# The first projection stage takes its column pairs in another order: q and k first instead of v first

## What is computed

```python
def rope(x, pos):
    ...
    x1, x2 = xf[..., :half], xf[..., half:]
    return jnp.concatenate([x1 * cos - x2 * sin, x1 * sin + x2 * cos], axis=-1).astype(x.dtype)

def retention_layer(h, s0, pos, w_in, head_norm, w_out):
    proj = h @ w_in
    qk = RET_HEADS * RET_DK
    q = proj[..., :qk].reshape(b, L, RET_HEADS, RET_DK)
    k = proj[..., qk:2 * qk].reshape(b, L, RET_HEADS, RET_DK)
    v = proj[..., 2 * qk:2 * qk + RET_VW].reshape(b, L, RET_HEADS, RET_DV)
    gate = proj[..., 2 * qk + RET_VW:]
    q = rope(q, pos)
    k = rope(k, pos) * (RET_DK ** -0.5)
    o, s_new = chunked_linear_recurrence(q, k, v, log_a, s0)
    ...
    return (o * jax.nn.silu(gate)) @ w_out, s_new
```

## Time and profile before

| | |
|---|---|
| median of 3 runs | 2247.02 us (2246.4 to 2247.16) |
| profiled execution | 2246.4 us, its span 2244.6 us |
| PE busy | 2090.1 us, 93% of the span |
| DVE busy | 1264.9 us, 56% |
| ACT busy | 857.7 us, 38% |
| POOL busy | 386.6 us, 17% |
| mean granted TensorE clock | 0.967 |

### The profile page before, as it was taken

How to read it: one execution, slowest core, us unless ns; L and a number is a source line. 1 busy time by engine, 2 the same in 40 slices (tenths; PEclk the granted TensorE clock), 3 DMA queues, 4 the chain that set the end, 5 groups by cost and what they waited for, 6 DMA issues and landing times. The chain is left out here.

```text
span 2244.6 us, 41786 instructions
## 1 busy us (share of the span) xinstructions
PE 2090.1 (93%) x14150; PEld 1899.2 (85%) x14150; DVE 1264.9 (56%) x1894; ACT 857.7 (38%) x1905; POOL 386.6 (17%) x566
## 2 busy tenths in 40 slices
PE   6999999998899997999689999999999999967998
PEld 6999999998666765888488999999999999855886
DVE  7755899674333355232244758575767767573331
ACT  7212112332223244232244545454554545464331
POOL 0200000000222120000001424343333434320000
PEclk9999999999999998999899999999999999978999
DMA  4433243332878787343512333333333332355340
GB/s 128 136 97 112 84 116 96 109 106 70 260 232 263 236 302 252 90 127 106 141 45 71 81 80 87 88 85 84 85 83 89 90 83 79 91 182 161 103 127 29
DMA packets 388688, 274.09 MB, mean 122 GB/s; under 512 B 119761, under 2 KB 344241, under 8 KB 388457
## 3 DMA queue, kind: packets, MB, share of 16 engines
q1 hardware_dynamic: 340342, 242.77, 37.0%
q10 hardware_dynamic: 48144, 28.76, 4.2%
HBM read 184.59 MB, written 86.88 MB: 121 GB/s over the span
## 5 line engine op out<-in xcount | busy, mean ns | idle before, releaser
L1514 PE MATMUL p3acc_ps<-xn2hi,p3whi 128*128 128x272 f32 x1536 | 463.2, 302 | 20.4 <-DVE xn2lo L2228 14.2
L1514 PE MATMUL p3acc_ps<-xn2lo,p3whi 128*128 128x272 f32 x1536 | 447.4, 291 | 0.0
L1514 PE MATMUL p3acc_ps<-xn2hi,p3wlo 128*128 128x272 f32 x1536 | 447.2, 291 | 0.0
L261 PE MATMUL p1ps<-x1hi,w1hi 128*128 128x272 f32 x1288 | 373.0, 290 | 4.7 <-issue 3.1
L261 PE MATMUL p1ps<-x1hi,w1lo 128*128 128x272 f32 x1288 | 372.8, 289 | 0.0
L261 PE MATMUL p1ps<-x1lo,w1hi 128*128 128x272 f32 x1288 | 371.8, 289 | 0.0
L1514 PEld LDWEIGHTS p3acc_ps<-xn2hi,p3whi 128*128 128x128 f32 x1536 | 294.1, 191 | 21.7 <-DVE xn2lo L2228 14.4
L1514 PEld LDWEIGHTS p3acc_ps<-xn2lo,p3whi 128*128 128x128 f32 x1536 | 294.4, 192 | 0.2
L1514 PEld LDWEIGHTS p3acc_ps<-xn2hi,p3wlo 128*128 128x128 f32 x1536 | 293.8, 191 | 0.0
L261 PEld LDWEIGHTS p1ps<-x1hi,w1hi 128*128 128x128 f32 x1288 | 243.3, 189 | 5.1 <-issue 5.1
L261 PEld LDWEIGHTS p1ps<-x1hi,w1lo 128*128 128x128 f32 x1288 | 243.7, 189 | 0.0
(11 more groups left out here) (297 smaller groups left out, 4151.2 us busy)
## 6 DMA issues: line engine op xcount, KB each, us to landing
w1raw<-in_ret_w_in SPq DMA_DIRECT2D x48, 512.0 KB, 5.0
p3raw<-in_ssm_w_in SPq DMA_DIRECT2D x48, 512.0 KB, 4.5
ret_vg<-y1out SPq DMA_DIRECT2D x32, 512.0 KB, 3.2
r_vg<-ret_vg SPq DMA_DIRECT2D x32, 512.0 KB, 4.3
r_sin<-in_state_ret SPq DMA_DIRECT2D x32, 512.0 KB, 5.9
out_ret_sample<-r_sout ACTq DMA_DIRECT2D x32, 512.0 KB, 5.8
s_cr<-sums SPq DMA_DIRECT2D x64, 256.0 KB, 3.3
ret_qk<-y1out SPq DMA_DIRECT2D x16, 512.0 KB, 3.7
```

What stands on the lines that cost most here:

```text
L261: last = nc.tensor.matmul(bank[:, 2 * at + i, 0:HB], w[s][:, idx, k, :], x[:, idx, k, i * HB:(i + 1) * HB], start=(k == 0 and j == 0), sto ...
L1514: last = nc.tensor.matmul(pr_ps[:, n % 2, 0:TB], wt[:, j % 2, k, :], x[:, k, b * TB:(b + 1) * TB], start=(k == 0 and i == 0), stop=(k == K ...
```

## The change

The kinds now stand in the order of the weights' columns: rope, copy, gate. The conversion `COLS` and the offset `ROPE` fall away. Since pairs 0 and 1 are now rope pairs, the rotation of pair 0 (both halves) and of the second half of pair 1 is put at the end of DVE's `second_pair`, with the wait for the tables; the first half of pair 1 comes by `finish_last` of the next pair. `over_pairs` writes 5 double pairs out, where it was 7, and the loops run longer (2, 3 and 2 rounds, where it was 1, 2 and 2).

```diff
-    kinds = ["copy"] * (INNER // P // 2) + ["rope"] * (RH * RDK // P) + ["gate"] * (INNER // P // 2)
-    ROPE = kinds.index("rope")
-    COLS = {"copy": 2 * RH * RDK // P, "rope": -2 * ROPE, "gate": 0}
+    kinds = ["rope"] * (RH * RDK // P) + ["copy"] * (INNER // P // 2) + ["gate"] * (INNER // P // 2)
...
-            last = PAIRS // 2 - 1
-            for v in range(last + 1):
+            for v in range(PAIRS // 2):
...
-                peeled = v < 2 or kind != prev or v == last or kinds[u + 2] != kind
-                if peeled:
+                if v < 2 or v == PAIRS // 2 - 1 or kind != prev:
...
-                    end = next(e for e in range(v, last + 1) if e == last or kinds[2 * e + 2] != kind)
+                    end = next(e for e in range(v, PAIRS // 2) if e == PAIRS // 2 - 1 or kinds[2 * e] != kind)
...
-                        sp.dma_start(raw[:, j, :, :], w_v[:, :, bass.ds((2 * u + j + COLS[kind]) * P, P)]).then_inc(raw_in, 16)
+                        sp.dma_start(raw[:, j, :, :], w_v[:, :, bass.ds((2 * u + j) * P, P)]).then_inc(raw_in, 16)
...
-                            sp.wait_ge(roped, 2 * (u - ROPE) + 2)
+                            sp.wait_ge(roped, 2 * u + 2)
...
                     take_c22(1, 1, 6, 2)
                     take_c21(1, 1, 3, 3)
                     low(2, 0, SPLIT[3:7])
+                    dma_wait(dve, tables_in, 2)
+                    rope(0, 0, 1)
+                    rope(0, 0, 0)
+                    rope(1, 1, 1)
...
                     if kind == "rope":
-                        if isinstance(u, int) and u == ROPE:
-                            dma_wait(dve, tables_in, 2)
                         rope(u, s, 1)
```

More of the change, by code:

```diff
@@ L206, in load_x, with load_raw @@
                         sp.dma_start(xin[n - a:b - a, t % XB, :], sample[n - SEQ:b - SEQ, :]).then_inc(x_in[t], 16)
-                def load_raw(u, kind):
+                def load_raw(u):
                     for j in range(2):
-                        sp.dma_start(raw[:, j, :, :], w_v[:, :, bass.ds((2 * u + j + COLS[kind]) * P, P)]).then_inc(raw_in, 16)
+                        sp.dma_start(raw[:, j, :, :], w_v[:, :, bass.ds((2 * u + j) * P, P)]).then_inc(raw_in, 16)
                 def store(u, v, s, kind):
@@ L221, in store @@
                         if kind == "rope":
-                            chunks, rows = (x[bass.ds(u - ROPE, 1), ..., j, :] for x in qk_out)
+                            chunks, rows = (x[bass.ds(u, 1), ..., j, :] for x in qk_out)
                         else:
@@ L235, in pair @@
                         sp.wait_ge(raw_done, u + 2)
-                        load_raw(u + 2, kinds[u + 2] if isinstance(v, int) else kind)
+                        load_raw(u + 2)
                 sp.dma_start(ident[:, :], A["ident"]).then_inc(ident_in, 16)
@@ L242, in _ @@
                 load_x(2)
-                load_raw(0, kinds[0])
+                load_raw(0)
                 for t in range(XB, NT):
@@ L246, in _ @@
                 sp.wait_ge(raw_done, 1)
-                load_raw(1, kinds[1])
+                load_raw(1)
                 sp.wait_ge(s1_raw, 2)
@@ L598, in rope @@
                 def rope(u, s, half):
-                    n = 2 * (u - ROPE) + (0 if half else 1)
+                    n = 2 * u + (0 if half else 1)
                     if not isinstance(u, int) or n:
```

## The result

The changed kernel takes 2262.85 us (median of 4 runs, 2261.09 to 2264.79) beside 2246.75 us for the kernel before (4 runs, 2246.4 to 2247.16): ratio 1.0072, 95% interval 1.0054 to 1.0089. It is slower by 16 us. The forecast was 2259.3 us with a range of 2256.0 to 2263.6. The profiled execution is not one of the four; it took 2265.41 us, its span 2263.6.

The account below looks back on a forecast made before the run. PE, busy 93% of the span, was taken to bound the kernel. A 10.4 us wait plus 1.9 us of clock loss, 12.3 us, on 2246.4 gave 2258.7, plus 0.6 to the runs' median: 2259.3 us, range 2256.0 to 2263.6.

Parts of the forecast that it names:

- The mechanism's own range: Whole kernel: 10.4 us of waiting plus 1.5 to 2.6 us of clock loss, 2258.9 to 2260.0 us; chance 0.78.
- the second stall: Rival: PE held again at A22 or S4 of pair 2, or in pair 3; 4.2 us more, 2263.5; chance 0.09.
- What bounds the stage: Steady pairs: PE is busy throughout, in copy and rope pairs alike at 21.1 us, so order gains nothing there.
- (a): S2 of pair 2: three rotations ahead of c12 of pair 1 make it start 10.4 us late.
- (b): Behind the gap at S2: PE runs at half clock for a while; 1.9 us lost, bounds 1.5 and 2.6.
- (c): Behind the gap, pair 3's weights and DVE's later results: no further PE wait; cost 0, upper bound 4.2 us.
- (d): Tables for the rotation: landed by 64 us, 20 us before the first rotation; cost 0.
- (e): Pairs 8 to 15 become copy pairs, losing 7.96 us of DVE's work each; PE's time unchanged, 0.
- Swallowed at the stage's end: Rival: PE's 14.5 us idle at the stage's end absorbs the delay, 2247.0 us; 0.04 together with an unseen gain.
- Theory A: Experiments' theory, behind the stage: further loss is the clock, varying between executions, 0 to 7 us; no chance given.
- Rival B: Experiments' rival: the order itself costs something, in the stage or behind it by a fixed amount; no chance given.

Follow-up runs that it names:

- e4: Changed kernel without the three rotations ahead of c12 of pair 1, semaphores counted up instead (part of q wrong): 2249.67 us, ratio 1.0010.
- e8: The changed kernel run a third time, no edit: 2263.01 us, ratio 1.0071 to the kernel before.
- e6: Changed kernel with 84 extra, useless matmuls between A11 and S2 of pair 2, keeping PE busy in the gap: 2256.35 us, ratio 1.0043.
- e5: Changed kernel with the three rotations of pairs 0 and 1 moved behind c12 of pair 1: 2258.28 us, ratio 1.0051.
- e1: The changed kernel run again, no edit: 2262.05 us, ratio 1.0058 to the kernel before.
- e2: Kernel before, old order, with 17 extra vector instructions where the change puts its rotations: 2261.3 us, ratio 1.0052.
- e9: Same kernel as e2 (old order with 17 extra vector instructions), run again: 2261.29 us, ratio 1.0062.
- e3: Kernel before with 17 extra vector instructions ahead of c12 of the stage's last pair: 2259.49 us, ratio 1.0048.
- e7: Kernel before with DVE's list at pair 1 reordered, u2 and u3 ahead of pair 2's weight sums and low rests: 2243.93 us, ratio 0.9989.

## Why the prediction was right, and where not

- *The range* held, but not by its own reasoning. The mechanism's own range was 2258.9 to 2260.0 us, and the median of 2262.85 lies 2.9 us above it. It lies within 2256.0 to 2263.6 only because the upper end was set by the second stall (2263.5), and that stall did not come. What the full range covered in its place was a part of the time that the sum did not have: that was luck. (The two ends are also not quite what the text adds up: 2257.4 - 0.3 is 2257.1, and 2263.5 + 0.3 is 2263.8.)
- *What bounds the stage* was right. PE is full in rope and copy pairs alike (21.10 of 21.10 us in pair 4 after), and e4 shows that their order costs the stage nothing.
- *(a) 10.4 us at S2.* Measured 10.5. The rotations take 4.30 us one after another where 4.35 were assumed, c12 came at 97.01 instead of 97.56; A11 ended 0.6 us sooner than in the trace before (87.25 against 87.84 for its last matmul), so the difference stood. All five traces with the stall show 10.4 to 10.7 us.
- *(b) 1.9 us of clock.* 2.6 us in the first trace, 12.4 + 0.6 - 10.5 = 2.5 by the sum, and 11.85 - 0.1 - 10.4 = 1.4 in e8 (A11 ended 0.1 us later than before there, and S2 started 10.4 us behind it); the bounds were 1.5 and 2.6, so the smallest value lies just below them. e6 makes it nothing. The Trainium skill (TensorE: Matmul & The Clock Gate, "What's actually happening") puts the ramp below 1% of a typical kernel span and advises against fitting it. The loss of 2.6 us is 0.1% of this span, as it says, but a fifth of the change. By that advice the stage would lose 10.4 us, and e6, where PE does not go idle, is the kernel that loses that (10.5). The Trainium skill says in the section "HAM oscillation — how this bites in real kernels" of the same page that after a long idle gap the next work starts cold; the row at 98.23 (0.43 us) and the window behind the gap (clock 0.50) agree.
- *(c) No second stall.* DVE waited 0.32 us for the raw weights (0 to 1 expected), u2(2) started at 104.99 (some 105.2 to 106.2 expected), and PE shows no further wait. (The 4.0 to 6.0 us to landing were those of the loads in pair 9 alone. Over the whole stage of the kernel before they were 3.8 to 9.7, so the bound of 103.5 was less sure than it looked. And 96.3 + 4.0 is 100.3, not 101.) In e5 DVE waited 1.17 us for the same load, and there it was on the path.
- *(d), (e) Tables and the freed pairs:* nothing in the stage, as e4 shows for all of it.
- *Swallowed at the stage's end:* no; the gap is 14.3 us and moved.
- *What was missing* is a term: what lies behind the stage was put at exactly nothing, with 0.3 us for the spread of runs. It is 3.3 +- 1.2 us on the means. The step that failed is the sentence that adds the sum of 12.3 us to one execution's time as if the rest were fixed: the three runs given lay within 0.8 us, and I took their closeness for the spread, where 47 runs of the kernel before range over 12 us.

What the part behind consists of is shown only in part, and it is not the clock alone. The windows from the next stage's first matmul to the end of the span, before, after, e1 and e8, hold the same 10014 matmuls:

```profile
564.70:2244.60 1679.90, 1562.57 (x10014) 1374.36 (x10014) 861.35 (x1301) 695.33 (x1604) 373.05 (x558) 0.96 0.43 127
```
```profile
576.89:2263.60 1686.71, 1568.02 (x10014) 1377.73 (x10014) 861.87 (x1301) 694.64 (x1604) 371.90 (x558) 0.96 0.43 127
```
```profile
576.77:2260.40 1683.63, 1562.92 (x10014) 1373.10 (x10014) 861.57 (x1301) 694.65 (x1604) 371.98 (x558) 0.96 0.44 127
```
```profile
576.36:2259.10 1682.74, 1568.31 (x10014) 1378.34 (x10014) 862.27 (x1301) 694.53 (x1604) 371.07 (x558) 0.96 0.43 127
```

Of the 6.8 us that this stretch is longer after, PE is busy for 5.4 us more and idle for 1.4 us more. In e1, the same program, of 3.7 us only 0.3 us are busy time and 3.4 us are idle time; in e8 PE is busy for 5.7 us more and idle for 2.9 us less. (A matmul's end is modelled, so the split is rough.) Slower matmuls can account for what came behind in the trace after and in e8, but not in e1, whose waits for DVE are longer than those of the kernel before: 22.9 us instead of 21.3 on s_sout and 15.0 instead of 14.2 on xn2lo. Theory A, which put all of it down to the clock, is not shown.

One place recurs. The windows of the next stage's first steps, after and before (the same work lies 12 to 14 us later after):

```profile
592.00:595.00 3.00, 3.00 (x6) 1.36 (x5) 0.07 (x1) 1.75 (x4) 0.00 (x0) 0.51 0.63 223
600.00:603.00 3.00, 3.00 (x15) 1.96 (x14) 2.08 (x3) 0.99 (x2) 1.84 (x3) 1.00 0.67 255
```
```profile
579.80:582.80 3.00, 3.00 (x10) 1.70 (x9) 1.28 (x1) 1.16 (x3) 0.00 (x0) 1.00 0.39 154
```

A stretch at half clock there is in all five traces with the stall (after, e1, e2, e8, e9), and not in before, e3, e4 and e5; but e6 and e7 have it too, so the stall is not its condition. Stretches late in the second layer differ between two traces of one kernel (e1). Which executions get which stays open.

Rival B, a fixed cost of the new order behind the stage, is neither shown nor excluded. For every kernel the third part can be reckoned alike: the mean of its runs less that of the kernel before beside it, less the amount by which the stage's end moved in its trace (for e3, the 12.3 us of delay). The first row and that of e2 and e9 are taken against all 47 runs of the kernel before. The errors are again twice the standard error of the means and leave out the spread of the stage's end.

| kernel | order | third part, us |
|---|---|---|
| changed (all runs) | new | 3.3 +- 1.2 |
| e4, less three rotations | new | 1.8 +- 1.9 |
| e5, c12 first | new | 4.3 +- 1.7 |
| e6, PE kept busy | new | -0.2 +- 2.2 |
| e2 and e9, stall | old | 1.4 +- 1.6 |
| e3, delay at the stage's end | old | -0.2 +- 1.6 |
| e7, DVE's list reordered | old | 1.4 +- 1.7 |

The new order leans to the larger values, which speaks for a B of 1 to 3 us; e6, which has the new order and nothing behind, speaks against it. Telling them apart would take more runs of e4 and e6 beside the kernel before.

## What to carry to other kernels

Read from the trace where an engine that is mostly idle is nevertheless late, and put no work ahead of the instruction that the busy engine waits for next: 12.9 us of rotations, put where 0.4 + 2.1 us were to spare, cost 10.4 us of waiting, while the two rotations of each steady rope pair cost nothing. Here a wait of the busy engine of 8 to 11 us was followed by a clock bill of 1.4 to 2.6 us that belongs into the sum. Where a forecast is to be good to 0.2%, take the spread of the whole program from many executions; three that agree within 0.8 us may be three out of a spread of 12.

## What the runs showed that was not expected

A wait that the profile puts down to "issue" can be a plain wait for another engine: the 3.1 us ahead of S4 ended 0.11 us after DVE's u3 and went when u3 was moved (e7). And the kernel before, whose first runs agreed within 0.8 us, ranged from 2240.77 to 2252.82 us over 47 runs, with the clock of the same window at 0.53 in one and 0.83 in another trace of one program (the changed kernel and e1).
